# Expert weights read in longer rows, and the down weights in runs of two rows, in a fused two-block network on one core

## The reference, cut to what matters

```python
def expert_choice_ffn(h, w_router, b_router, w_gate, w_up, w_down):
    cap = (EC_CAPACITY_FACTOR * S) // N_EXPERTS                      # 64
    affinity = jax.nn.softmax((h @ w_router + b_router).astype(jnp.float32), axis=-1)
    gates, idx = lax.top_k(affinity.transpose(0, 2, 1), cap)
    xin = h[bidx, idx]
    hid = jax.nn.silu(jnp.einsum('becd,edf->becf', xin, w_gate)) * jnp.einsum('becd,edf->becf', xin, w_up)
    y = jnp.einsum('becf,efd->becd', hid, w_down) * gates[..., None].astype(h.dtype)
    return jnp.zeros_like(h).at[bidx, idx].add(y)
```

## Time and profile before

| | us |
|---|---|
| median of 3 runs | 2862.34 |
| lowest, highest | 2862.19, 2865.59 |
| the profiled execution | 2864.15 |
| its span, first to last instruction | 2862.3 |
| PE busy, share of the span | 2583.3, 90% |
| DVE busy | 1028.3, 36% |
| ACT busy | 586.4, 20% |
| read from HBM | 590.54 MB |
| queue of SP, its share of 16 engines' span | 581.14 MB, 56.6% |
| expert stage, first weight load to the end | 1795 to 2862.3 |

### The profile page before, as it was taken

One profiled execution on the slowest core, in us unless ns is written; L12 is line 12 of the kernel. 1 busy time (PEld: TensorE's weight loads), 2 busy tenths in 40 slices (PEclk: granted clock), 3 DMA queues, 4 the chain that ended last, 5 costly groups with the idle time before them and its releaser, 6 DMA issues.

```text
span 2862.3 us, 23705 instructions
## 1 busy us (share of the span) xinstructions
PE 2583.3 (90%) x9887; PEld 1392.3 (49%) x9887; DVE 1028.3 (36%) x1703; ACT 586.4 (20%) x912; POOL 54.1 (2%) x75
## 2 busy tenths in 40 slices
PE   7999998899999799999999899797879797888888
PEld 2444544468888468888555374332323232322322
DVE  3353355245664566564347661300101011010101
ACT  1111125142233152233324251200000000000000
POOL 2000000000000200000100000000000000000000
PEclk9999999899999899999999999899999999999999
DMA  8040240035554135553110000899999999999998
GB/s 319 12 165 22 71 156 9 30 132 177 177 191 146 45 118 191 199 183 119 35 59 30 20 33 1 323 387 387 387 387 386 387 387 387 387 386 387 387 387 314
DMA packets 299233, 594.23 MB, mean 208 GB/s; under 512 B 12450, under 2 KB 13984, under 8 KB 298998
## 3 DMA queue, kind: packets, MB, share of 16 engines
q1 hardware_dynamic: 295170, 581.14, 56.6%
q0 software_dynamic: 3648, 11.44, 1.2%
q10 hardware_dynamic: 308, 0.13, 0.0%
HBM read 590.54 MB, written 2.13 MB: 207 GB/s over the span
## 4 chain that ended last, share of the span: by engine, by line
PE 70%; DMA 20%; DVE 7%; ACT 3%; issue 1%; SPq 0%; ACTq 0%; DVEq 0%
PE PS L610 12%; PE PS L783 8%; PE PS L785 8%; PE PS L784 8%; PE PS L149 7%; DMA RING<-in_w_up_dram 6%; PE PS L1007 6%; PE PS L989 5%; DMA RING<-in_w_gate_dram 4%; DMA XT<-in_w_up_dram 2%; PE PS L1017 2%; PE PS L555 2%; PE PS L519 2%; DMA AT_e<-in_w_gate_dram 2%; DMA XT<-in_w_gate_dram 2%; PE PS L686 1%
## 5 line engine op out<-in xcount | busy, mean ns | idle before, releaser
L989 PE MATMUL PS<-RING,HID_e 128*64 128x512 f32 x1280 | 349.0, 602 | 76.6 <-DMA RING<-in_w_gate_dram 44.9
L989 PEld LDWEIGHTS PS<-RING,HID_e 128*64 128x64 f32 x1280 | 104.9, 137 | 284.5 <-issue 153.3
L2093 DVE TENSOR_TENSOR TMP<-TMP,PS 128x512 f32<-128x512 f32 x32 | 22.0, 688 | 609.2 <-PE PS L989 609.2
L1485 DVE SCALAR_TENSOR_TENSOR TMP<-RING,MODC,TMP 128x512 f32<-128x512 f32 x224 | 168.4, 752 | 19.0 <-ACT TMP L1094 10.0
L1007 PE MATMUL PS<-RING,HID_e 128*64 128x512 f32 x632 | 156.5, 594 | 5.5 <-DMA RING<-in_w_down_dram 5.5
L610 PE MATMUL PS<-AT_a,RING 128*128 128x512 f32 x320 | 139.0, 593 | 0.0
L1416 ACT ACTIVATE HID_e<-PS 128x512 f32<-128x512 f32 x32 | 19.1, 597 | 545.4 <-PE PS L519 545.4
L989 PE MATMUL PS<-AT_e,HID_e 128*64 128x512 f32 x296 | 105.8, 599 | 19.6 <-DMA AT_e<-in_w_gate_dram 11.4
L989 PE MATMUL PS<-XT,HID_e 128*64 128x512 f32 x312 | 109.4, 599 | 14.6 <-DMA XT<-in_w_gate_dram 12.8
L610 PE MATMUL PS<-AT_e,RING 128*128 128x512 f32 x256 | 111.9, 593 | 0.0
L783 PE MATMUL PS<-AH_b,WH_b 128*128 128x512 f32 x256 | 101.6, 397 | 3.2 <-DVE AL_b L1523 3.2
(11 more groups left out here) (416 smaller groups left out, 4071.1 us busy)
## 6 DMA issues: line engine op xcount, KB each, us to landing
RING<-in_w_up_dram SPq DMA_DIRECT2D x81, 1024.0 KB, 14.2
RING<-in_w_gate_dram SPq DMA_DIRECT2D x79, 1024.0 KB, 14.4
RING<-in_w_down_dram SPq DMA_DIRECT2D x79, 1024.0 KB, 14.3
RING<-in_mlp_w_dram SPq DMA_DIRECT2D x64, 1024.0 KB, 5.4
RING<-in_ada_w_dram SPq DMA_DIRECT2D x48, 1024.0 KB, 5.3
RING<-in_w_ada_dram SPq DMA_DIRECT2D x24, 1024.0 KB, 5.1
AT_e<-in_w_down_dram SPq DMA_DIRECT2D x21, 1024.0 KB, 14.2
XT<-in_w_gate_dram SPq DMA_DIRECT2D x20, 1024.0 KB, 14.4
```

The source lines that it names most:

```text
L989: last = pe.matmul(b[64 * d:64 * d + 64, :], xv_[:, k, 64 * d:64 * d + 64], ring.view("gu", n, fg, m, k // 4, d)[:, k % 4, :], start=k == ...
L1485: dve.scalar_tensor_tensor(out=ada_tmp, in0=ring.view("ada", which, cb, k // 4)[:, k % 4, :], scalar=sil[:, c0 + step * k:c0 + step * k + ...
```

## The change

The weights are asked for in longer contiguous pieces; number (48 a round) and size (1 MiB) of the loads, and the 13 slots, stay.

Gate and up: a load now holds two blocks of 128 matrix rows instead of four, and of each row 1024 columns instead of 512: pieces of 4096 bytes. PE therefore fills two banks (groups fg = 2 half and 2 half + 1) at a time: for each block k, the four matmuls of two banks and two experts. Gate of both groups comes first, then up of both.

Down: a load holds, per partition, two whole matrix rows that lie next to each other in memory, one piece of 8192 bytes. In a half of 1024 matrix rows, partition p gets rows 8p to 8p+7, so block k consists of the matrix rows 8p + k and not of 128 adjacent ones. The hidden columns have to match: the transposes read the two groups' products as one run of 1024 columns (`hidden`, the two buffers of TMP) and take every eighth column, starting at k. A turn can thus only come when both groups of its half are there. Each block k of down is multiplied into both banks before the next.

The turns move: 0 and 1 stand together behind the second half's gate matmuls, 2 and 3 behind the first four blocks of down. ACT's copies move with them, and the two buffers of TMP are bound to even and odd fg.

```diff
+        hidden = TMP[:, 0:2, :].rearrange("p a b -> p (a b)")
...
-                for fg in range(4):
+                for half in range(2):
                     for m, nm in enumerate(("w_gate_2", "w_up_2")):
-                        for kh in range(2):
+                        for kp in range(4):
                             for d in range(2):
-                                ring.load(sp, w, ("gu", n, fg, m, kh, d), rows_of(A[nm][0, 2 * n + d], 4 * kh, 512 * fg),
-                                          (4, 512), (T_moe, "gu", n, fg, m, kh))
-                for kg in range(4):
-                    for hf in range(2):
-                        for d in range(2):
-                            ring.load(sp, w, ("dn", n, kg, hf, d), rows_of(A["w_down_2"][0, 2 * n + d], 4 * kg, 512 * hf),
-                                      (4, 512), (T_moe, "dn", n, kg, hf))
+                                ring.load(sp, w, ("gu", n, half, m, kp, d),
+                                          rows_of(A[nm][0, 2 * n + d], 2 * kp, 1024 * half, 2, 1024), (2, 1024),
+                                          (T_moe, "gu", n, half, m, kp))
+                for kp in range(8):
+                    for d in range(2):
+                        rows8 = A["w_down_2"][0, 2 * n + d].rearrange("(h p k) n -> h p k n", h=2, k=8)
+                        ring.load(sp, w, ("dn", n, kp, d), rows8[kp // 4, :, 2 * (kp % 4):2 * (kp % 4) + 2, :],
+                                  (2, 1024), (T_moe, "dn", n, kp))
...
-            w.wait_ge(*V_moe.at("act", n, fg))
-            q = act_tmp.of("hid", n, fg)
-            transposes(pe, b, [q[:, j * 128:(j + 1) * 128] for j in range(4)]).then_inc(*T_moe.up("hid", n, fg))
+            w.wait_ge(*V_moe.at("act", n, fg | 1))
+            transposes(pe, b, [hidden[:, 4 * (fg % 2) + j::8] for j in range(4)]).then_inc(*T_moe.up("hid", n, fg))
...
+            for half in range(2):
+                fgs = (2 * half, 2 * half + 1)
+                for m in range(2):
...
                     for k in range(8):
-                        for d in range(2):
-                            w.wait_ge(*ring.landed("gu", n, fg, m, k // 4, d))
-                            last = pe.matmul(b[64 * d:64 * d + 64, :], xv_[:, k, 64 * d:64 * d + 64],
-                                             ring.view("gu", n, fg, m, k // 4, d)[:, k % 4, :], start=k == 0, stop=k == 7)
-                        if k % 4 == 3:
-                            last.then_inc(*T_moe.up("gu", n, fg, m, k // 4))
-                    if m == 0 and fg:
-                        pe_moe_turn(pe, w, n, fg - 1)
+                        for c, b in enumerate(bs):
+                            for d in range(2):
+                                w.wait_ge(*ring.landed("gu", n, half, m, k // 2, d))
+                                wv = ring.view("gu", n, half, m, k // 2, d)[:, k % 2, 512 * c:512 * (c + 1)]
+                                last = pe.matmul(b[64 * d:64 * d + 64, :], xv_[:, k, 64 * d:64 * d + 64], wv,
+                                                 start=k == 0, stop=k == 7)
+                        if k % 2:
+                            last.then_inc(*T_moe.up("gu", n, half, m, k // 2))
+                    if half and m == 0:
+                        pe_moe_turn(pe, w, n, 0)
+                        pe_moe_turn(pe, w, n, 1)
...
-            for kg in range(4):
-                if kg == 1:
+            for k in range(16):
+                w.wait_ge(*S_moe.at("hid", n, k // 4))
+                for hf, b in enumerate(bs):
+                    for d in range(2):
+                        w.wait_ge(*ring.landed("dn", n, k // 2, d))
+                        wv = ring.view("dn", n, k // 2, d)[:, k % 2, 512 * hf:512 * (hf + 1)]
+                        last = pe.matmul(b[64 * d:64 * d + 64, :], hidT[:, k, 64 * d:64 * d + 64], wv,
+                                         start=k == 0, stop=k == 15)
+                if k % 2:
+                    last.then_inc(*T_moe.up("dn", n, k // 2))
+                if k == 3:
+                    pe_moe_turn(pe, w, n, 2)
                     pe_moe_turn(pe, w, n, 3)
...
-                    q = act_tmp.take(w, ("hid", n, fg), (T_moe, "hid", n, fg))
-                    w.wait_ge(*T_moe.at("gu", n, fg, 0, 1))
-                    if fg:
-                        act_moe_hidden(act, w, n, fg - 1)
+                    q = act_tmp.seat(w, fg % 2, ("hid", n, fg), (T_moe, "hid", n, fg | 1))
+                    w.wait_ge(*T_moe.at("gu", n, fg // 2, 0, 3))
+                    if fg > 1:
+                        act_moe_hidden(act, w, n, fg - 2)
...
+                act_moe_hidden(act, w, n, 2)
                 act_moe_hidden(act, w, n, 3)
```

More of the change, by code:

```diff
@@ L981, in pe_up @@
             w.wait_ge(*S_moe.at("xt", n, 1))
[L982 to L985, removed]
-                    for k in range(8):
-                        for d in range(2):
-                            w.wait_ge(*ring.landed("gu", n, fg, m, k // 4, d))
-                            last = pe.matmul(b[64 * d:64 * d + 64, :], xv_[:, k, 64 * d:64 * d + 64],
-                                             ring.view("gu", n, fg, m, k // 4, d)[:, k % 4, :], start=k == 0, stop=k == 7)
-                        if k % 4 == 3:
-                            last.then_inc(*T_moe.up("gu", n, fg, m, k // 4))
-                    if m == 0 and fg:
-                        pe_moe_turn(pe, w, n, fg - 1)
+            for half in range(2):
+                fgs = (2 * half, 2 * half + 1)
+                for m in range(2):
+                    bs = [banks.take(w, ("up" if m else "gate", n, fg), *(((V_moe, "act", n, fg),) if m else
+                                                                         ((S_moe, "silu", n, fg),))) for fg in fgs]
+                    for k in range(8):
+                        for c, b in enumerate(bs):
[9 more added lines that the diff above has]
+                        pe_moe_turn(pe, w, n, 1)
@@ L996, in pe_down @@
         def pe_down(pe, w, n):
             bs = [banks.take(w, ("down", n, hf), (V_moe, "y", n, hf)) for hf in range(2)]
-            for kg in range(4):
-                if kg == 1:
-                    pe_moe_turn(pe, w, n, 3)
[L1001 to L1009, removed]
+            for k in range(16):
[10 more added lines that the diff above has]
+                    pe_moe_turn(pe, w, n, 2)
+                    pe_moe_turn(pe, w, n, 3)
@@ L1407, in act_gather @@
             if n >= 2:
-                w.wait_ge(*T_moe.at("gu", n - 2, 3, 1, 1))
+                w.wait_ge(*T_moe.at("gu", n - 2, 1, 1, 3))
             act.activation(xins[x][:, 4:8, :], banks.of("xt", n, 1).rearrange("p (k n) -> p k n", n=128), ACT.Copy,
@@ L1414, in act_moe_hidden @@
             if n:
-                w.wait_ge(*T_moe.at("dn", n - 1, 3, 1))
+                w.wait_ge(*T_moe.at("dn", n - 1, 7))
             act.activation(hidT[:, 4 * fg:4 * fg + 4, :], banks.of("hid", n, fg).rearrange("p (k n) -> p k n", n=128),
@@ L2091, in dve_experts @@
                     w.wait_ge(*S_moe.at("silu", n, fg))
-                    w.wait_ge(*T_moe.at("gu", n, fg, 1, 1))
+                    w.wait_ge(*T_moe.at("gu", n, fg // 2, 1, 3))
                     dve.tensor_tensor(q, q, banks.of("up", n, fg), ALU.mult).then_inc(*V_moe.up("act", n, fg))
@@ L2098, in dve_experts @@
                 w.wait_ge(*S_moe.at("g2b", 1))
-                w.wait_ge(*T_moe.at("dn", n, 3, 1))
+                w.wait_ge(*T_moe.at("dn", n, 7))
                 if n:
```

## The result

| | before | after |
|---|---|---|
| median, same chip (4 runs each), us | 2863.2 | 2817.72 |
| lowest, highest | 2862.19, 2865.59 | 2815.47, 2818.96 |
| span of the profiled execution | 2862.3 | 2813.7 |
| from one scatter to the next, mean of six rounds | 130.7 | 124.5 |

The ratio is 0.9839 with a 95% interval of 0.9822 to 0.9856: faster, by 45.5 us. The forecast was 64.3 us and its range ended at 2812. Span against span it is 48.6 us, so 15.7 us of the forecast are missing there.

The account below looks back on a forecast made before the run. DMA bound the expert stage at 387 GB/s, 48 loads a round. Faster loads save 65.3 us, less 1 us for the ring in PE's pause: 64.3 us off 2862.3 gives 2798 us, range 2787 to 2812.

Parts of the forecast that it names:

- The price of a row: Weight loads: rows of 4096 bytes cost 160 ns, 2.56 us a load; rows of 8192 bytes 310.6 ns, 2.485 us.
- The 65.3 us: Expert stage, from load 14 on: 243 gate and up loads save 36.5 us, 128 down loads 28.8 us.
- the 3.5 ns of the prediction: Fixed cost of a packet by the Trainium skill, 3 cycles: by that rule 24.5 us saved, 2838 us.
- The ring in PE's pause: After a round's last up pair, until matmuls free slots: 13 loads bridge 29.3 us, 1.7 us remain; 1 us charged.
- Rival (b): PE's pauses outlast 13 faster loads by 2 us in each of six rounds, 12 us come back: 2810; chance 0.08.
- The sign that the prediction had named for a wrong pause: In the slices of a round, a DMA gap before the first down pair; no size given.
- PE's order, DVE and ACT: Expert stage: reordered matmuls, strided transposes, products and copies cost nothing; PE needs 108.6 us of a 121.7 us round.
- (a): Down loads: rows of 8 KB pay no more than rows of 4 KB, 55.7 us saved, 2806.6 us; chance 0.17.
- (c): Gate and up loads: the 4 KB window shows a burst, not the rate; 19.5 us saved, 2843; chance 0.05.
- (d): All loads: the rate is set by something rows do not change, HBM or address pattern: 2862; chance 0.03.
- (e): Expert stage: PE becomes the bound through a throttled clock, at 0.75 118 us slower, 2980; chance 0.04.
- The Trainium skill's warning of large pitches between partitions: Down loads, row pitch growing from 4 to 32 KiB: mildest loss 3%, 10 us, about 2808; no chance given.

Follow-up runs that it names:

- the late kernel: Against after, the gather moved from before the down matmuls to behind down block 3, with turns 2 and 3 in its place: 2803.44 us, 0.9789.
- the wide kernel: Against the late kernel, gate and up loads also in rows of 8192 bytes, all four turns behind the scatter: 2782.34 us, 0.9713.

## Why the prediction was wrong

**The price of a row: right.** The windows give 410 and 421 GB/s, so 2.557 and 2.491 us a load, where 2.56 and 2.485 were forecast; 2.71, 2.557 and 2.491 us lie on one line to about 0.01 us. The 65.3 us were nearly all there to be had: 6 rounds of the late kernel are 2750.14 - 2016.34 = 733.8 us, against 784.3 of before, 8.4 us each, and its whole time is 61.0 us less than before's (2864.39 to 2803.44). The Trainium skill, "DMA: Bandwidth & Descriptors", section "iDMA fabric", and its 408.7 GB/s for 4 KiB rows agree with the 410 of the window. The fixed part of a row is 2 x 84.7 - 159.8 = 9.6 ns by these windows; the same page's section "Why small descriptors are slow" puts it at 3 cycles a packet, the 3.5 ns of the prediction, and these windows contradict it.

**"The ring in PE's pause": this step failed.** It found 5.6 us queued ahead less 1 for starting, 4.6 us to spare before the change and 1.7 after, and charged 1 us for everything. The table has +2.7 and -1.3. Three parts made the difference:

- From the least landing time of 8.3 us it took off the load's own 2.7 us and called the rest queue. But that landing is the last engine's. The queue of the mean engine was 1.9 us shorter, and in the landing moments of before the last engine does report 1.9 us behind the mean. The trace of before showed it where the last load of all ends: the slices over 2838 to 2848 (0.25 us each) fall from full to nothing over 5 us, twice the 2.7 us of a load.

```profile
DMA  9999999999997666655555555542111111000000
```

- The lead grew with the change: 0.97 MB at 387 GB/s are 2.5 us, 1.61 MB at 421 are 3.8 us. 1.3 us, which no step had. (By the landing moments, 1.9 and 3.1 us.)
- The 2.9 us for 13 faster down loads were right. 2.7 - 2.9 - 1.3, and 0.2 for slightly shorter pauses, are the -1.3.

And the step priced a dry spot at the missing time, "a few", 1 us in all. It comes in every pause and costs 2.3 us where 1.3 are missing, since the engines ahead of the mean are dry for longer and the late ones then stand at the first gate loads: seven pauses are 16 us. 64.3 + 1 - 16 = 49.3 us; the span shrank by 48.6. (The median's 45.5 is less, since the other executions of after are up to 3.5 us longer than the profiled one, its fastest, while before's profiled one is 1 us above its median.)

**Rival (b) had the mechanism**, a pause that outlasts the ring by 2 us in each of six rounds, 2810, with a chance of 0.08. It was the likely case: 1.7 us of spare, with an error of that size in how it was read, was no cover. The sign that the prediction had named for a wrong pause, a gap before the first down pair, came too: it lies at 2038.4 to 2041.6, and the pair is done at 2040.7.

**PE's order, DVE and ACT: right.** Eight strided transposes take 1.09 us (L521 x8 above), where four took 0.59: no loss. PE waits for DVE as before, and for loads 39.7 and 27.8 us against 30.9 and 44.9, so loads still come last. Waits of after (engine, line, releaser: total, times, longest):

```profile
PE PS L993 <- DMA RING<-in_w_up_dram: 39.7, 29, 1.5
...
PE PS L993 <- DMA RING<-in_w_gate_dram: 27.8, 20, 1.5
PE PS L149 <- DVE HID_e L2040: 27.7, 7, 4.5
```

```profile
SPq L132 <- PE PS L1009: 246.4, 50, 21.0
SPq L132 <- PE PS L993: 203.4, 93, 5.6
```

SP's wait on the down matmuls, up to 21.0 us at a time, is the pause, and in after it is no longer harmless: the engines have nothing left at its end. The time behind the last landing is 15.4 us as before (2798.27 to 2813.7).

**The other rivals fell:** (a), since down loads run at 421; (c), since 410 holds over 60 us; (d), since each part alone gains; (e), since PE waits for loads throughout, and gets a clock of 0.98 over the six rounds. The Trainium skill's warning of large pitches between partitions ("DMA: Bandwidth & Descriptors", section "Latency and other measured facts") begins at 512 KiB, above this case: at a pitch of 32 KiB the down loads run at 421, no slower than the wide kernel's other rows.

## What to carry to other kernels

A load has landed when the last of 16 engines has ended; the buffer that bridges a pause must be judged by the mean engine and those ahead of it, which were one to two loads further on here. Speeding the loads up shortens that same buffer: with every gain in rate, ask how long the consumer's longest pause between freeing two slots is, and shorten the pause rather than add slots: a step that frees nothing belongs behind the first steps that do. Test the parts of a change one by one; where two are whole alone and not together, look for a buffer that both draw on.

## What the runs showed of the hardware

- A row costs 9.6 ns and 75.1 ns for each 2 KB of it, from 2 KB to 8 KB: 387, 410 and 421 GB/s on one core.
- Loads in longer rows land later after their issue, though nothing waits longer for them. The last up loads take 14.2 us in before, 18.5 in after, and in the wide kernel 26.1 us:

```profile
1982.34 26.09 DMA RING<-in_w_up_dram
```

  These are 5.2, 7.2 and 10.5 loads at their rates, with the same 13 slots: SP gets further ahead with its requests when they consist of fewer rows.
- All 16 engines take the same time for a load, but they are out of step, and by more when the loads of a round have rows of 4 KB: 1.61 MB ahead in after, 2.02 with 14 slots, 1.30 with 4 KB rows for gate and up alone, but 0.97 with 2 KB, 0.94 with 2 and 8 KB, and 0.87 with 8 KB throughout. The landing moments show where the gap opens: in the loads just after the queue has run empty. In the run-in, from the 14th to the 18th load, the first and last engine part to 5.5 us where gate rows have 4 KB (after, late), but only to 1.8 in before and 1.6 in the wide kernel; in steady stretches it changes only by single steps of one engine, 1.6 us at most. Why 4 KB rows do this is open: nothing here tells rows from addresses.
- PE's granted clock was 0.83 over the 20 us in which it stood idle for 3.9 us between scatter and gather, and 1.00 where the transposes and down matmuls filled that place. Of the two levels it was the lower, 1.2 GHz, from the end of the idle time into the gather:

```profile
2024.60:2031.20 6.60, 4.94 (x6) 2.19 (x7) 1.61 (x9) 0.00 (x0) 0.00 (x0) 0.50 1.01 422
```
